# A two-layer decoder trunk: the down projection of its MLP as seven block products instead of eight

## The reference, cut to what matters

```
h2 = rms_norm(x, ln_mlp_pre)
ff = jnp.square(jax.nn.relu(h2 @ w_up)) @ w_down
return x + rms_norm(ff, ln_mlp_post)
```

## Time and profile before

| | |
|---|---|
| median of 3 runs | 1902.08 us (1900.87 to 1903.65) |
| span of the profiled execution | 1901.8 us |
| PE busy | 1881.2 us, 99% of the span |
| PEld busy | 1525.0 us, 80% |
| DVE busy | 1140.6 us, 60% |
| ACT busy | 491.9 us, 26% |
| POOL busy | 350.8 us, 18% |
| DMA | 186.78 MB, mean 98 GB/s |
| chain that ended last | PE 95%, ACT 2%, DVE 1% |

### The profile page before, as it was taken

The page is one execution under the profiler, slowest core; times in us unless marked ns, Lnnn a source line. Parts: engine busy times, 40 slices in busy tenths (PEclk is TensorE's granted clock), DMA queues, the critical chain, the costliest instruction groups (busy, mean ns, idle before and its releaser), DMA issues.

```text
span 1901.8 us, 24979 instructions
## 1 busy us (share of the span) xinstructions
PE 1881.2 (99%) x8814; PEld 1525.0 (80%) x8814; DVE 1140.6 (60%) x1920; ACT 491.9 (26%) x967; POOL 350.8 (18%) x549
## 2 busy tenths in 40 slices
PE   8999999999999999999999999999999999999998
PEld 6877767888788888888878767678888888888887
DVE  5855789753476542453478558888434765325534
ACT  3163352421334100011221633524122331000101
POOL 2221111111220222222112211111112202222220
PEclk9999999999999999999999999999999999999999
DMA  6432123322521332222222321132225223222221
GB/s 240 137 123 83 67 67 97 84 67 78 202 98 45 122 100 99 90 99 100 78 89 89 133 72 67 67 99 71 78 78 220 68 78 101 98 100 100 90 98 56
DMA packets 73053, 186.78 MB, mean 98 GB/s; under 512 B 18368, under 2 KB 30848, under 8 KB 72064
## 3 DMA queue, kind: packets, MB, share of 16 engines
q1 hardware_dynamic: 41904, 152.10, 23.5%
q10 hardware_dynamic: 31056, 33.38, 5.2%
HBM read 174.40 MB, written 11.06 MB: 98 GB/s over the span
## 4 chain that ended last, share of the span: by engine, by line
PE 95%; ACT 2%; DVE 1%; issue 1%; DMA 0%; DVEq 0%; SPq 0%; ACTq 0%
PE psD L1099 24%; PE psD L1101 24%; PE psD L1100 24%; PE psM L1100 4%; PE psM L1101 4%; PE psM L1099 4%; PE psM L1158 2%; PE psM L1172 1%; PE psM L1367 1%; PE psM L1165 1%; PE psM L1385 1%; PE psM L1264 1%; PE psM L1373 1%; PE psM L1256 1%; ACT wide L1611 1%
## 5 line engine op out<-in xcount | busy, mean ns | idle before, releaser
L1099 PE MATMUL psD<-a_hi,w_hi 128*128 128x512 f32 (+2 forms) x1488 | 594.6, 400 | 0.8 <-DVE w_lo L1009 0.6
L1101 PE MATMUL psD<-a_hi,w_lo 128*128 128x512 f32 (+2 forms) x1488 | 575.2, 387 | 0.0
L1100 PE MATMUL psD<-a_lo,w_hi 128*128 128x512 f32 (+2 forms) x1488 | 574.2, 386 | 0.0
L1009 DVE TENSOR_TENSOR w_lo<-raw,w_hi 128x1024 fp32r<-128x1024 f32 x208 | 253.9, 1221 | 290.1 <-POOL w_hi L1077 289.4
L1099 PEld LDWEIGHTS psD<-a_hi,w_hi 128*128 128x128 f32 (+1 forms) x1488 | 279.1, 188 | 76.1 <-issue 21.3
L1076 POOL TENSOR_TENSOR w_hi<-raw,tabs 128x1 fp32r<-128x1 f32 x272 | 60.9, 224 | 1512.7 <-PE psD L1101 1288.4
L1100 PEld LDWEIGHTS psD<-a_lo,w_hi 128*128 128x128 f32 (+1 forms) x1488 | 279.4, 188 | 57.3 <-issue 4.3
L1101 PEld LDWEIGHTS psD<-a_hi,w_lo 128*128 128x128 f32 (+1 forms) x1488 | 278.8, 187 | 57.8 <-issue 0.2
L1077 POOL TENSOR_SCALAR w_hi<-raw 128x1023 fp32r<-128x1023 f32 x272 | 298.5, 1098 | 0.0
L1884 ACT CAST f_hi<-gt 128x512 f32 x64 | 39.8, 622 | 476.0 <-DVE gt L2321 470.7
L2318 DVE TENSOR_SCALAR gt<-psD 128x512 f32<-128x512 f32 x64 | 44.2, 691 | 133.0 <-PE psD L1101 133.0
(11 more groups left out here) (273 smaller groups left out, 2577.2 us busy)
## 6 DMA issues: line engine op xcount, KB each, us to landing
raw<-in_ws SPq DMA_DIRECT2D x272, 512.0 KB, 3.2
s_raw<-in_wo ACTq DMA_DIRECT2D x14, 512.0 KB, 11.5
x<-rows_d ACTq DMA_DIRECT2D x4, 1024.0 KB, 5.6
x<-out ACTq DMA_DIRECT2D x2, 2048.0 KB, 8.0
e_raw<-in_wo ACTq DMA_DIRECT2D x8, 512.0 KB, 6.6
tabs<-in_tab SPq DMA_DIRECT2D x1, 2944.0 KB, 11.5
x<-in_x SPq DMA_DIRECT2D x4, 512.0 KB, 6.7
out<-x SPq DMA_DIRECT2D x4, 512.0 KB, 7.5
```

The source lines that it names most:

```text
L1009: dve.tensor_tensor(w_lo[:, s, :], raw[:, s, :], w_hi[:, s, :].bitcast(F32), ALU.subtract) \
L1099: pe.matmul(out, lhi, rhi, start=start, stop=False)
L1100: pe.matmul(out, lhi, rlo, start=False, stop=False)
L1101: return pe.matmul(out, llo, rhi, start=False, stop=stop)
```

## The change

The down projection of a layer is done in four chunks of 1024 hidden rows (8 tiles, `CT`), each as one 2 x 2 block product after Strassen in Winograd's form. Token tiles 0, 1 against 2, 3 are the two block rows of F; even against odd hidden tiles are its two block columns; the two halves of the output columns split w_down. A chunk has seven products of half size instead of eight. Each is two steps of 12 matmuls of 128 x 512 (2 token tiles x 2 contraction tiles x 3 passes), so 14 steps (`STEPS`); before, the same rows took 8 slabs of 24 matmuls.

```
+                    def combine(c, p):
+                        first = 4 * (c * PAIRS + p)
+                        pool.wait_ge(*on("f_sq", c * CT + 2 * p + 2))
+                        pool.tensor_tensor(fr[:, S1, :], fr[:, A21, :], fr[:, A22, :], ALU.add).then_inc(*inc("comb"))
+                        pool.tensor_tensor(fr[:, S3, :], fr[:, A11, :], fr[:, A21, :], ALU.subtract).then_inc(*inc("comb"))
+                        pool.wait_ge(*on("comb", first + 1))
+                        pool.tensor_tensor(fr[:, S2, :], fr[:, S1, :], fr[:, A11, :], ALU.subtract).then_inc(*inc("comb"))
+                        pool.wait_ge(*on("comb", first + 3))
+                        pool.tensor_tensor(fr[:, S4, :], fr[:, A12, :], fr[:, S2, :], ALU.subtract).then_inc(*inc("comb"))
...
+                    for c in range(CHUNKS):
+                        for i in range(CT):
+                            n = layer * NSLAB + SL_MLP + c * CT + i + 2
+                            if n < DEPTH * NSLAB:
+                                round_(n)
+                            if i % 2:
+                                combine(c, i // 2)
+                            if i >= CT - 2:
+                                t1(c, i - CT + 2)
+                        t2(c, 0)
+                        t3(c, 0)
+                        t2(c, 1)
+                        t4(c, 0)
+                        t3(c, 1)
+                        t4(c, 1)
...
+                    def relu(c, i):
+                        act.wait_ge(*on("slab_done", SL_MLP + c * CT + i + 1))
+                        if i % 2 == 0 and c * CT + i:
+                            act.wait_ge(*on("f_loB", (c * CT + i) // 2))
...
+                    def f_square(c, i):
+                        dve.wait_ge(*on("relu_up", c * CT + i + 1))
+                        sig(dve.tensor_tensor(f_pair(i), f_pair(i), f_pair(i), ALU.mult), "f_sq")
+
+                    def f_rest(c, p, part):
+                        w = slice(A11, S1) if part == "A" else slice(S1, A21)
+                        dve.wait_ge(*on("f_hi" + part, c * PAIRS + p + 1))
+                        if part == "A":
+                            own("f_sq")
+                        sig(dve.tensor_tensor(f_lo[:, p, w, :], fr[:, w, :], f32(f_hi[:, p, w, :]), ALU.subtract), "f_lo" + part)
+
+                    def d_rest(c, st):
+                        hi, lo = operand(c, st)
+                        dve.wait_ge(*on("d_hi", c * NSTEP + st + 1))
+                        operand_free(dve, c, st)
+                        sig(dve.tensor_tensor(lo, source(st), f32(hi), ALU.subtract), "d_lo")
...
+                    AFTER = {2: "P1", 3: "P2", 5: "P5", 7: "P6", 9: "P3", 11: "P7", 13: "P4"}
+                    for c in range(CHUNKS):
+                        for i in range(CT):
+                            if i % 2 == 0 and i:
+                                f_rest(c, i // 2 - 1, "B")
+                            f_square(c, i)
+                            if i < CT - 1:
+                                ahead(c, i)
+                            if i % 2:
+                                f_rest(c, i // 2, "A")
+                            elif i:
+                                d_rest(c, i // 2 - 1)
+                        f_rest(c, PAIRS - 1, "B")
+                        ahead(c, CT - 1)
+                        for st in range(NSTEP if c < CHUNKS - 1 else WHOLE):
+                            if st in AFTER:
+                                dve.wait_ge(*on("d_done", c * NSTEP + st + 1))
+                                evict_product(c, AFTER[st])
+                            if st + RING < NSTEP:
+                                d_rest(c, st + RING)
```

More of the change, by code:

```diff
@@ L576, in slab_plan @@
     add("out0", *(("out", i, 2, 0, S) for i in range(0, STAYING[0][1], 2)))
[L577 to L580, removed]
+    add("up", *(("up", 0, KT, i * P, P) for i in range(FF // P)))
     return number, holds
@@ L741, in build @@
         with ExitStack() as mlp:
[L742 to L747, removed]
+            f_hi = sb("f_hi", [P, PAIRS, 7, S // 2], F32R, where=mlp)
+            f_lo = sb("f_lo", [P, PAIRS, 7, S // 2], F32R, where=mlp)
+            d_hi = sb("d_hi", [P, RING, SLAB], F32R, where=mlp)
+            d_lo = sb("d_lo", [P, RING, SLAB], F32R, where=mlp)
+            d_raw = sb("d_raw", [P, len(DOWN_SLOT), SLAB], where=mlp)
         psD = [ctx.enter_context(nc.psum_tensor(f"psD{i}", [P, S], F32)) for i in range(4)]
@@ new lines, in product @@
+                    def product(c, st, tt):
+                        q, j = STEPS[st]
+                        a, _, bank = PRODUCTS[q]
+                        hi, lo = operand(c, st)
+                        out = banks[bank][tt][:, :]
+                        for k in range(2):
+                            w = slice(k * S, (k + 1) * S)
+                            ins = passes(out, f_hi[:, 2 * j + k, a, cut(tt)], f_lo[:, 2 * j + k, a, cut(tt)], hi[:, w], lo[:, w],
+                                         q in ("P1", "P2", "P5", "P4") and j == k == 0, j == k == 1,
+                                         q in ("P3", "P6", "P7"))
+                        return ins
@@ new lines, in halves2 @@
+                    def halves2(t, half, evicted):
+                        act.wait_ge(*on("evict", 16 * (CHUNKS - 1) + evicted))
+                        squares("post_mlp", t, half, wide[:, t, half * S:(half + 1) * S])
+                    for c in range(CHUNKS):
+                        for i in range(CT):
+                            if i % 2 == 0 and i:
+                                f_halves(c, i // 2 - 1, "B")
+                            relu(c, i)
+                            if i % 2:
+                                f_halves(c, i // 2, "A")
+                            elif i:
+                                d_high(c, i // 2 - 1)
+                        f_halves(c, PAIRS - 1, "B")
+                        for st in range(RING, NSTEP if c < CHUNKS - 1 else 10):
+                            d_high(c, st)
+                            if c == CHUNKS - 1 and st == 7:
+                                for t in range(2):
+                                    halves2(t, 0, 3 + t)
```

453 lines of the change are left out of this document (259 added, 194 removed).

## The result

| | before | after |
|---|---|---|
| median | 1901.91 us (1900.87 to 1903.65, 4 runs) | 1981.81 us (1980.59 to 1982.69, 4 runs) |
| span of the profiled execution | 1901.8 us | 1980.2 us |
| PE busy, share of the span | 99% | 95% |
| POOL busy | 350.8 us | 635.5 us |
| chain that ended last, PE's share | 95% | 67% |

The ratio is 1.0416, 95% interval 1.0403 to 1.0428: the change makes the kernel 80 us slower. Forecast were +52, with a range from 1876 to 1986.

What follows compares the result with a forecast made beforehand. The prediction took PE's matmuls to bound the kernel, busy 99% of the span. With a chunk at 90.4 us, 1901.8 + 20 (six chunks) + 22 (last chunks) + 10 (tails) gave 1954 us, range 1876 to 1986.

Steps and rivals of the forecast that it cites:

- The break-even and what is removed: Both layers' down projections: 192 fewer matmuls at 0.2267 us save 43.5 us; break-even at 5.4 us of new waits per chunk.
- The turns: DVE operations with two SBUF inputs and POOL's SBUF-reading ones alternate by whole instructions; a chunk waits 8.8 us, six chunks +20.
- turns cost little: Rival, chance 0.17: two-input POOL work and DVE run side by side, only step 3 late by 1.0 us; 1878 us.
- POOL's two-input price: POOL's sums and differences in the MLP chunks: 2.05 us for 1024 columns, 0.65 for 256.
- more is lost: Rival, chance 0.21: clock falls after step 3's wait (+14, 1968) or POOL's two-input work costs more (+20, 1974); both 1988.
- twice the reads: Pricing of POOL's two-input work: twice the one-input 0.91 ns a column plus 0.19 us, 2.05 us for 1024 columns.
- Places: PE's waits in a chunk: up slabs 4 and 6 0.5, 0.9 us; steps 2, 3, 7 1.4, 3.9, 1.5; steps 8, 9 0.3 each.
- the chunk by hand: One chunk followed from up slab 1's end: slab 4 starts at 11.2 for 10.72 us; whole chunk 90.4, 3.35 over before.
- Step 7: Seventh down step of a chunk: needs three POOL differences in a row, alternating with DVE, so PE waits 1.5 us.
- The last chunk and the tails: Each layer's last chunk takes 98 us, two of them +22; tails +6 in layer 0 and +4 in layer 1.
- The clock as an added loss: After step 3's wait of 3.9 us the clock could fall to 1.2 GHz, 1.7 us each, +14, 1968 us.

Runs made afterwards that it cites:

- experiment 11: Against the change: sums and differences moved from POOL to DVE, square read from PSUM, down-step rounding and splits reordered; 1887.65 us, ratio 0.9921.
- experiment 3: Against the change: POOL's sums and differences replaced by MEMSETs of the same size that read nothing, output not the reference's; 1874.85 us, ratio 0.9855.
- experiment 4: Against the change: PE does 8 unread matmuls ahead of step 2's wait and 13 ahead of step 3's; 1982.77 us, ratio 1.0418.
- experiments 2: Against the change: POOL's sums and differences replaced by one-input multiplications by 1 of the same size, output not the reference's; 1885.16 us, ratio 0.9908.
- 1 to 3: The first of these, against the change: the square takes its second factor from PSUM in place of SBUF; 1963.67 us, ratio 1.0329.
- experiment 8: Against the change: sums on DVE, square from PSUM, step 3's rounding and split first, P5's first step ahead of P1's second; 1934.42 us, ratio 1.0163.

## Why the prediction was right, and where it was off

- **The break-even and what is removed: right.** 192 matmuls at an unchanged pace; a chunk without waits takes 81.9 us in experiment 11, forecast 81.6.
- **The turns: right as the mechanism.** With POOL's sums and differences reading nothing the change is 28 us faster than the kernel before (experiment 3), so they make the whole of the loss. How much of that is turns and how much POOL's own length is an estimate, some 10 to 2 of a chunk's 12.8 us (behind experiment 3). That the rival *turns cost little* had given 1878 and experiment 3 measured 1874.85 says nothing for that rival's sum: it reckoned with POOL's two-input prices, and the MEMSETs are shorter. A wide two-input operation on POOL, which no row of before showed, takes turns too: at 846.72 rest B is ready, POOL's difference ends at 847.95, and rest B ends 1.08 us after that.
  The Trainium skill ("SBUF — State Buffer", Who interferes with whom) has the rule, and the trace agrees.
- **POOL's two-input price: the term that was mis-sized.** Taken were 2.05 and 0.65 us, measured without a hold 2.38 (at 845.57) and 0.73 to 0.74. The forecast priced this at some 20 us in *more is lost*, which is close to the 24 that the six chunks cost over the forecast.
  The estimate of 2.35 from the Trainium skill's table ("GPSIMD Engine Reference", section 3.1) comes out if the figure for 2048 columns is halved above a fixed part of 0.19; the trace agrees with it rather than with twice the reads.
- **Places: right.** Up slabs 4 and 6, steps 2, 3, 7, 8 and 9 wait, and nothing else in a chunk does; sums take 0.74 to 1.65, squares 1.15 on average where 1.2 had been said for a held one. Up to slab 4 the chunk by hand is right to 0.06 us until POOL's sums come in a row, and the trace is 0.25 to 0.4 later from there on.
- **Step 7: the largest part of the miss in a chunk.** 1.5 us forecast, 2.8 by experiment 4; the 1.3 of the trace are what slow matmuls had left over. That the trace's 1.3 is near the forecast's 1.5 is chance. Step 7 with the slow matmuls before it (+1.4), steps 2 (+0.7) and 3 (+0.5), four other places (+0.3 each) and the remainders (+0.2) make 12.8 for 8.8.
- **The last chunk and the tails.** 101.1 and 98.4 us against 98, tails +7 and +3 against +6 and +4: the forecast's 32 us are 35.
- **The clock as an added loss: refuted.** *More is lost* gave +14 us for it. The clock fell as it said, and already after step 2's wait, for 3.4 or 6.8 us at a time, but a chunk whose time is set by the chain through POOL didn't get longer by it (experiment 4, and the two chunks of 94.4 us with different clocks).

In short, +44 for the six chunks in place of +20 is nearly all of the miss of 28 us. That POOL's two-input work beside DVE's is the source is shown by experiments 2, 3 and 11, that DVE's two-input operations lose turns to POOL by 1 to 3; how the loss divides between holds and POOL's own length is worked out from the trace and was not tried.

## What to carry to other kernels

A second engine is little help for a job that must take turns with the first: before work goes from DVE to POOL, count the operands that each operation on both sides reads from SBUF, and price a lost turn at the full length of the longest operation on the other side. In a chain of such turns the parts don't add up, because each long operation left holds whatever now stands beside it; take them all away (here 94 us) before judging one (18, 31, 21). And where a wait and a low clock stand side by side, keep PE busy once: if the time stays, the chain that ended the wait is the bound and not the clock.

## What the runs showed of the hardware that was not expected

- DVE and POOL, both with queued operations that read two operands from SBUF, alternated instruction by instruction, whatever their lengths: operations of 0.42 us took 2.46 to 2.62 beside ones of 2.4 (experiment 8).
- POOL's writing alone held nothing: beside its MEMSETs DVE's down split took 1220 ns, as alone. Beside one-input operations it took 1323, beside two-input ones, twice as long themselves, 1701. The square stays at 1149 ns even in experiment 3, since POOL's rounding, which reads, still stands beside it.
- PE's granted clock fell to 1.2 GHz for 3.4 or 6.8 us after waits of 2 to 4 us, 37 us in layer 0 in all, and in a chunk it cost nothing that could be measured; in the endings that wasn't tried.
